# Head norms of a two-layer block: sums in four column groups of TensorE, roots read back from four row groups

## The reference

```python
z = h @ w_in[l]
q_lat, kv_lat, k_rope, mla_gate, conv_in, conv_gate = jnp.split(z, splits, axis=-1)
q = (rms_norm(q_lat, q_lat_g[l]) @ w_q_up[l]).reshape(b, s, N_HEADS, QK_DIM)
...
k = jnp.concatenate([k_nope, k_rope_h], axis=-1)
q = rms_norm(q, q_norm_g[l])
k = rms_norm(k, k_norm_g[l])
q = jnp.concatenate([q[..., :NOPE_DIM], apply_rope(q[..., NOPE_DIM:], cos, sin)], axis=-1)
k = jnp.concatenate([k[..., :NOPE_DIM], apply_rope(k[..., NOPE_DIM:], cos, sin)], axis=-1)
attn = causal_block_attention(q, k, v).reshape(b, s, D_MLA)
```

## Time and profile before

| What | Value |
|---|---|
| Median of 3 runs | 2063.28 us (2061.64 to 2065.86) |
| Profiled execution, its own time | 2066.0 us |
| Its span | 2064.2 us |
| Mean granted TensorE clock | 0.994 |
| PE, weight loads, DVE, ACT busy | 98%, 89%, 74%, 49% |

### The profile page before, as it was taken

One profiled execution on the slowest core, in us unless ns is written; L12 is line 12 of the kernel. 1 busy time (PEld: TensorE's weight loads), 2 busy tenths in 40 slices (PEclk: granted clock), 3 DMA queues, 4 the chain that ended last, 5 costly groups with the idle time before them and its releaser, 6 DMA issues.

```text
span 2064.2 us, 31575 instructions
## 1 busy us (share of the span) xinstructions
PE 2026.0 (98%) x13492; PEld 1833.6 (89%) x13492; DVE 1525.7 (74%) x2050; ACT 1015.3 (49%) x1388; POOL 0.2 (0%) x4
## 2 busy tenths in 40 slices
PE   7999999999999999999999899999999899999999
PEld 7999889889998888999888799898998799988987
DVE  5466665867878777788877568999756669999564
ACT  4373755454444344444434475444554655444642
POOL 0000000000000000000000000000000000000000
PEclk9999999999999999999999999999999999999999
DMA  6433334956888888888898445443345445443353
GB/s 248 145 142 123 134 112 164 332 201 248 327 324 328 335 336 336 301 327 325 324 345 331 175 143 180 153 172 125 117 153 186 149 166 184 143 147 130 107 201 122
DMA packets 63356, 440.69 MB, mean 213 GB/s; under 512 B 7152, under 2 KB 7408, under 8 KB 11760
## 3 DMA queue, kind: packets, MB, share of 16 engines
q1 hardware_dynamic: 61632, 433.86, 57.2%
q10 hardware_dynamic: 1584, 4.81, 0.6%
HBM read 436.55 MB, written 2.10 MB: 212 GB/s over the span
## 4 chain that ended last, share of the span: by engine, by line
PE 95%; DVE 3%; ACT 2%; DMA 0%; issue 0%; ACTq 0%
PE PS L516 18%; PE PS L517 17%; PE PS L518 17%; PE PS L463 11%; PE PS L464 11%; PE PS L462 10%; PE PS L454 9%; DVE WL L933 1%; PE PS L541 1%; ACT WH L1732 0%; DVE RAW L942 0%; DMA X<-in_x 0%; DVE Y L982 0%; DVE Y L929 0%; PE PS L782 0%
## 5 line engine op out<-in xcount | busy, mean ns | idle before, releaser
L933 DVE TENSOR_TENSOR WL<-RAW,WH 128x1024 fp32r<-128x1024 f32 (+1 forms) x636 | 762.8, 1208 | 447.2 <-ACT WH L1732 444.4
L1732 ACT ACTIVATE WH<-RAW 128x1024 fp32r<-128x1024 f32 (+1 forms) x636 | 658.8, 1047 | 819.3 <-PE PS L518 489.8
L516 PE MATMUL PS<-HTh,WH 128*128 128x256 f32 x2928 | 845.7, 289 | 2.5 <-DVE WL L933 1.0
L517 PE MATMUL PS<-HTl,WH 128*128 128x256 f32 x2928 | 830.7, 284 | 0.0
L518 PE MATMUL PS<-HTh,WL 128*128 128x256 f32 x2928 | 830.6, 284 | 0.0
L516 PEld LDWEIGHTS PS<-HTh,WH 128*128 128x128 f32 x2928 | 563.7, 193 | 25.3 <-issue 23.5
L517 PEld LDWEIGHTS PS<-HTl,WH 128*128 128x128 f32 x2928 | 564.1, 193 | 0.6
L518 PEld LDWEIGHTS PS<-HTh,WL 128*128 128x128 f32 x2928 | 563.5, 192 | 0.0
L942 DVE SCALAR_TENSOR_TENSOR RAW<-RAW,CB 128x2048 f32<-128x2048 f32 x96 | 219.3, 2284 | 0.0
L463 PE MATMUL PS<-WL,Uh 128*128 128x512 f32 x512 | 203.1, 397 | 0.0
L464 PE MATMUL PS<-WH,Ul 128*128 128x512 f32 x512 | 202.4, 395 | 0.0
(11 more groups left out here) (282 smaller groups left out, 1778.0 us busy)
## 6 DMA issues: line engine op xcount, KB each, us to landing
RAW<-in_w_in SPq DMA_DIRECT2D x112, 1024.0 KB, 4.8
RAW<-in_ada_w SPq DMA_DIRECT2D x96, 1024.0 KB, 5.7
RAW<-in_w_up SPq DMA_DIRECT2D x64, 1024.0 KB, 5.1
RAW<-in_w_down SPq DMA_DIRECT2D x64, 1024.0 KB, 6.0
RAW<-in_w_out SPq DMA_DIRECT2D x48, 1024.0 KB, 4.8
RAW<-in_w_pw SPq DMA_DIRECT2D x8, 1024.0 KB, 4.8
RAW<-in_w_in SPq DMA_DIRECT2D x8, 768.0 KB, 4.2
RAW<-in_w_q_up SPq DMA_DIRECT2D x6, 1024.0 KB, 4.8
```

The source lines that it names most:

```text
L516: e.matmul(out, sh, ah, start=first and i % 2 == 0, stop=False, skip_group_check=True)
L517: e.matmul(out, sh, al, start=False, stop=False, skip_group_check=True)
L933: e.tensor_tensor(m[f"WL{j % NHL}"][:, 0:nk * w], m[f"RAW{i % NRAW}"][:, k0 * w:(k0 + nk) * w], m[f"WH{j % NHL}"][:, 0:nk * w].bitcast(F32 ...
L1732: e.activation(m[f"WH{j % NHL}"][:, 0:nk * w], m[f"RAW{i % NRAW}"][:, k0 * w:(k0 + nk) * w], ACT.Copy).then_inc(signals["high"], 1)
```

## The change

The eight heads are laid over the array. Sums: head h goes to group h // 2 of the array's columns, that is to partitions 32 (h // 2) of the bank, row h % 2 there; its weights are 32 columns ("hot2"). Each step takes one head of the first four and one of the last four, so its two matmuls lie two groups apart (h = n - 1 and n + 3); ACT squares heads n and n + 4 of a use accordingly. The rotated part's sums are written to all four groups: four matmuls in both uses, where the key use had one. HS is then 128 partitions tall, and DVE's and ACT's three operations on it run over all of them. Roots: a matmul reads 32 rows of HS at partition 32 i, a row group of its own for each pair of heads, and writes to one bank for each pair. Two pairs are spread together in steps 6 and 8, the matmuls in the order pair i, pair i + 1, pair i, pair i + 1; steps 7 and 9 have none. DVE's steps 7 to 10 are as before, and it keeps two banks for each two pairs.

```diff
--- before.py
+++ after.py
@@ -57,7 +57,7 @@
     out = {}
     out["ident"] = np.eye(128)
     out["ones"] = np.ones((128, 128))
-    out["half0"] = np.repeat((p < 64)[:, None], 8, 1) * 1.0
+    out["half0"] = np.repeat((p < 64)[:, None], 32, 1) * 1.0
     rot = np.zeros((128, 128))
     for base in (0, 64):
         for i in range(32):
@@ -65,9 +65,10 @@
             rot[base + i, base + 32 + i] = 1.0
     out["rot"] = rot
     out["hot"] = np.repeat(np.arange(15)[None, :] == 7, 128, 0) * 1.0
-    hotr = np.zeros((128, 14))
-    hotr[:64, 6] = 1.0
-    hotr[64:, 7] = 1.0
+    out["hot2"] = np.repeat(np.arange(33)[None, :] == 1, 128, 0) * 1.0
+    hotr = np.zeros((128, 32))
+    hotr[:64, 0] = 1.0
+    hotr[64:, 1] = 1.0
     out["hotr"] = hotr
     t = q[:, None]
     dist = np.concatenate([t - p[None, :], t + 128 - p[None, :], t - p[None, :]], 1).astype(np.float64)
@@ -723,16 +724,16 @@
                     b = small()
                     course.held = b
                     pe.wait_ge("q_rope_sq", u + 1)
-                    for i in range(rope):
-                        hot = cn("hotr")[:, 6 - 2 * i:14 - 2 * i] if u % 2 else cn("half0")
-                        op = mm(b, 0, 256, hot, SQR[:, i, :], i == 0, False, slice(0, 8))
+                    for i in range(4):
+                        op = mm(b, 0, 256, cn("hotr" if u % 2 else "half0"), SQR[:, i if u % 2 else 0, :], True, False,
+                                slice(32 * i, 32 * i + 32))
                     op.then_inc(signals["h_rope_sum"], 1)
                 if 1 <= n < 5:
-                    i = n - 1
-                    pe.wait_ge("h_sq", 4 * u + i + 1)
-                    for h in (2 * i, 2 * i + 1):
-                        op = mm(b, 0, 256, cn("hot")[:, 7 - h:15 - h], VT[:, 2 * (i % 2) + h % 2, :], False, h == 7,
-                                slice(0, 8))
+                    pe.wait_ge("h_sq", 4 * u + n)
+                    for k, h in enumerate((n - 1, n + 3)):
+                        at, r = 32 * (h // 2), h % 2
+                        op = mm(b, 0, 256, cn("hot2")[:, 1 - r:33 - r], VT[:, 2 * ((n - 1) % 2) + k, :], False, r == 1,
+                                slice(at, at + 32))
                     op.then_inc(signals["h_sum"], 1)
                     free[b] = ("h_ms", 2 * u + 1)
                 for i in range(2 * n - 4, min(2 * n - 2, rope)) if n in (2, 3) else ():
@@ -743,15 +744,17 @@
                     free[r] = ("h_sin", 5 * L + turns - rope + i + 1)
                 if n == 5:
                     course.held = None
-                if 6 <= n < 10:
-                    i = n - 6
-                    r = small()
+                if n in (6, 8):
+                    pair = [small(), small()]
                     pe.wait_ge("h_ms", 2 * u + 2)
                     for k in range(2):
-                        op = mm(r, 256 * k, 256 * k + 256, ident[0:8, 2 * i + k:2 * i + k + 1].broadcast_to([8, 128]),
-                                HS[0:8, :], k == 0, k == 1)
-                    op.then_inc(signals["h_wide"], 1)
-                    free[r] = ("h_apply", 4 * u + i + 1)
+                        for i, r in enumerate(pair, n - 6):
+                            at = 32 * i
+                            op = mm(r, 256 * k, 256 * k + 256, ident[at:at + 32, at + k:at + k + 1].broadcast_to([32, 128]),
+                                    HS[at:at + 32, :], k == 0, k == 1)
+                            if k:
+                                op.then_inc(signals["h_wide"], 1)
+                                free[r] = ("h_apply", 4 * u + i + 1)
                 if u % 2 and n == 8:
                     flags.add(("scores", L))
                 yield
@@ -1382,27 +1385,31 @@
                         dve.wait_ge("h_wide", 4 * u)
                     else:
                         dve.wait_ge("r_wide", 4)
-                    e.tensor_scalar(HS[0:8, :], b[0:8, 0:256], 1.0 / (192 * scale * scale), EPS / (scale * scale),
+                    e.tensor_scalar(HS[:, :], b[:, 0:256], 1.0 / (192 * scale * scale), EPS / (scale * scale),
                                     ALU.mult, ALU.add).then_inc(signals["h_ms"], 1)
                     course.held = None
                     dve.wait_ge("h_rope", 2 * u + 1)
                     dve.wait_ge("h_sin", 5 * L + turns)
                     tt("h_rope", dst, dst, spare[:, 0:rope, :], ALU.add)
                     dve.wait_ge("h_root", u + 1)
-                    e.reciprocal(HS[0:8, :], HS[0:8, :]).then_inc(signals["h_ms"], 1)
+                    e.reciprocal(HS[:, :], HS[:, :]).then_inc(signals["h_ms"], 1)
+                if n == 9:
+                    wide = late
                 if n >= 7:
                     i = n - 7
                     dve.wait_ge("h_wide", 4 * u + i + 1)
                     dve.wait_ge("h_rope", 2 * u + 2)
                     n2 = flat(heads_[:, 2 * i:2 * i + 2, :])
-                    e.scalar_tensor_tensor(n2, n2, wide_gain, wide[:, :], ALU.mult, ALU.mult)
+                    e.scalar_tensor_tensor(n2, n2, wide_gain, wide[i % 2][:, :], ALU.mult, ALU.mult)
                     for lo in (0, 64):
                         src = m["QP"][:, i, :] if u % 2 else KV[:, 2, :]
                         op = e.tensor_tensor(parts[lo:lo + 64, i, :], src[lo:lo + 64, :],
-                                             wide[lo:lo + 64, 4 * lo:4 * lo + 256], ALU.mult)
+                                             wide[i % 2][lo:lo + 64, 4 * lo:4 * lo + 256], ALU.mult)
                     op.then_inc(signals["h_apply"], 1)
-                if 6 <= n < 10:
-                    wide = small()
+                if n == 6:
+                    wide = [small(), small()]
+                if n == 8:
+                    late = [small(), small()]
                 if u % 2 and n == 8:
                     flags.add(("scores", L))
                 yield
@@ -2000,7 +2007,7 @@
                     if n >= 2 or u % 2:
                         act.wait_ge("h_sum", 4 * u + n - 1)
                     e.activation(VT[:, 2 * (n % 2):2 * (n % 2) + 2, :],
-                                 m["QN" if u % 2 else "KN"][:, 2 * n:2 * n + 2, :], ACT.Square).then_inc(
+                                 m["QN" if u % 2 else "KN"][:, n:n + 5:4, :], ACT.Square).then_inc(
                         signals["h_sq"], 1)
                 if n == 1:
                     course.held = course.small_bank()
@@ -2009,8 +2016,9 @@
                 if n == 5:
                     course.held = None
                     act.wait_ge("h_ms", 2 * u + 1)
-                    e.activation(HS[0:8, :], HS[0:8, :], ACT.Sqrt).then_inc(signals["h_root"], 1)
-                if 6 <= n < 10:
+                    e.activation(HS[:, :], HS[:, :], ACT.Sqrt).then_inc(signals["h_root"], 1)
+                if n in (6, 8):
+                    course.small_bank()
                     course.small_bank()
                 if u % 2 and n == 8:
                     flags.add(("scores", L))
```

## The result

The changed kernel takes **2047.15 us** (median of 4 runs, 2044.48 to 2051.34); the kernel before, beside it, 2063.32 (2061.64 to 2065.86). The profiled execution took 2045.3 us, its span is 2043.5.

The account below looks back on a forecast made before the run. PE (98% busy) was taken as the bound, with DVE a second bound inside the norm stretch. PE's savings less waits for DVE gave 4.35 a layer, 8.7 us: 2063.3 to 2054.6 us, range 2051.5 to 2064.5.

Parts of the forecast that it names:

- passes start in queue order ... k matmuls take (k + 1)p: Norm matmuls on PE: a second pass overlaps only the next matmul's first; p is one pass, 0.216 us.
- PE alone: Time taken off PE's queue by sums and roots over both layers, before any waits for DVE: 12.5 us.
- rival A: Sums and roots on PE: both passes of neighbours in different groups overlap fully; -10.6 us, 2052.7 us; chance 0.08.
- Rival D: Sums and roots on PE: each change of group drains, 0.09 us, and hides nothing; +4.6 us, 2067.9 us; chance 0.13.
- What DVE gives back: PE's waits for DVE, per layer: 0.46 us lost at the gated values' half, 1.4 at the query roots' reciprocal.
- The net of the groups: Gain in the norm stretch after PE's waits for DVE: 4.35 us per layer, 8.7 for both.
- The constants grow by 75 columns: Larger constants ahead of weights on SP's queue: 37.5 KB more to transfer, taken as 0, at most 0.1 us.
- ops of DVE and ACT on 128 partitions: Norm operations on 128 partitions instead of 8 cost nothing: reciprocals 1753 ns against 1738, 0.02 us.

Follow-up runs that it names:

- extensions: Changed kernel with gated values first, plus norm work ahead of taps (2038.68 us), then four root pairs in one step (2038.5), then reciprocal before rope's last addition (2039.93).
- eight columns: Eight unused columns added behind the constants of the kernel before: 2056.39 us; with the gated values first as well, 2055.94 us.

## Why the prediction was wrong

It had the sign, the overlap and the kind of wait. Both were mis-sized, in opposite directions, and a third effect was put at nothing. By its own steps:

- **"passes start in queue order ... k matmuls take (k + 1)p": wrong.** Passes of different groups run side by side whatever their order in the queue. A sum step gives 0.40 and not 0.22, the first query step 1.69 and not 1.08, a pair of root steps 1.24 and not 1.02. PE alone: 18.9 us, not 12.5. This is rival A's mechanism (19.4 on PE, net 10.6); it was given 0.08 for the reason that "a matmul's second pass stands in the queue ahead of the next one's first", which the run with the roots in another order refutes. The Trainium skill, "TensorE: Matmul & The Clock Gate", Part 3, has such starts about 4 ns apart; the trace agrees in kind, with 6 to 7 ns. By that rule A was the case.
- **Rival D's price of a change of group:** none is seen. Starts in different groups lie 6 to 7 ns apart, where D wanted 0.09 us.
- **"What DVE gives back": the right engine, the wrong place.** The margin at the gated values was taken on the split behind them, 1.79 us, and 0.46 lost. The wait that ends last there is for the bank pair that L1646 reads. Its write ends at 1357.61 + 1.66 = 1359.27, and the first product into that pair stands in the trace of before at

```profile
1359.63 0.28 PE L516 MATMUL PS<-QLh,WH 128*128 128x256 f32 x1
```

so 0.36 of margin was there. Measured 2.44 lost there. At the query roots 1.4 was forecast; measured 0.80 in layer 1 and nothing in layer 2, since PE had by then already been held. The key roots (0.53) were not in the sum. Together 4.2 in layer 1, where 1.9 was forecast.
- **The net of the groups** was 4.35 a layer by forecast, 5.4 and 4.9 measured; 8.7 against 9.2 to 10.0 in all. That this is near is two errors that cancel: 6.4 us too little taken off PE, some 5 too little waited for. It is luck.
- **"The constants grow by 75 columns": the error that counts.** They were costed as a transfer, 0 to 0.1 us. That bytes in front move every tensor behind was not asked. It was worth 6.6 to 7.4 us, nearly all of the 7.5 between forecast and result; no rival held it, so the range could not either. The trace of before did show a sign, 512-column products 227 ns apart from HTh and 233 from Uh and Ul, same shape, same clock, but a weak one: those from AH and AL are 233 apart too and stayed so.
- **Right:** ops of DVE and ACT on 128 partitions cost nothing that can be seen (DVE's busy time 1525.7 before, 1524.5 after); no transfer became a bound.
- **Not foreseen:** the fall of the clock behind a wait, 1.5 us a time.

## What to carry to other kernels

Small matmuls in different row or column groups, f32 ones with their two passes too, cost as much together as the longest group alone; before counting that as time won, list for each point at which the engine gets earlier every thing it waits for there, the release of an output bank as well as the next operand. A size in the allocation is also an address for all behind it: compare the placement of much-read operands between two versions, and pad a new one back before its change is judged. When a faster engine meets a bound, look first at the order of the other engine's work: one write moved ahead of two others was worth nothing before and 6 to 7 us after; the changed kernel with it is the fastest here together with two of its extensions, 2038.5 to 2039.0 us.

## What the runs showed of the hardware

- Four row groups take sixteen f32 passes in 1.14 us, two take eight in 1.13, one takes four in 1.13.
- Issue order inside such a block does not matter: A0, A1, B0, B1 is as fast as A0, B0, A1, B1.
- With Uh and Ul 32 bytes off a multiple of 64, the 512-column products over them take 233 ns from start to start, on a multiple of 64 they take 229, at the 2.4 GHz level: 2%, in four kernels and both directions. Those over HTh and HTl, which did not move, did not change. Those over AH and AL moved alike and kept 233. So this is a finding on these products and not a rule for every moving operand; moving one tensor alone was not tried.
- Behind 10 of 12 waits of 2.1 us or more PE's clock fell to the 1.2 GHz level for some 3 us, at 1.5 us a time. In the five traces in which that wait is gone or 0.9 us long (roots apart, the changed kernel with the gated values first, and its three extensions) the clock is 1.00 throughout those places. A wait is not the only thing that stands ahead of such a fall: in the two runs of the kernel before with eight columns PE is busy for all of the 4.00 us ahead of it (1836 to 1840, and 1833 to 1837), with 22 and 21 matmuls.
